# The norm behind a mixture of experts, run under its last expert

## The reference

```python
def layer_norm(x, g, b):
    mu = jnp.mean(x, -1, keepdims=True)
    var = jnp.mean(jnp.square(x - mu), -1, keepdims=True)
    return (x - mu) * lax.rsqrt(var + LN_EPS) * g + b

def expert_choice_moe(x, w_router, w_gate_up, w_down):        # 16 experts, 128 tokens each
    aff = jax.nn.softmax(x @ w_router, axis=-1)
    gates, idx = lax.top_k(jnp.swapaxes(aff, 1, 2), cap)
    xs = x[bi, idx]
    g, u = jnp.split(jnp.einsum('becd,edf->becf', xs, w_gate_up), 2, axis=-1)
    out = jnp.einsum('becf,efd->becd', jax.nn.silu(g) * u, w_down) * gates[..., None]
    return jnp.zeros_like(x).at[bi, idx].add(out)

for layer in range(2):
    mix = windowed_gqa_sink(x, ...) if layer == 0 else bidir_rglru_block(x, ...)
    x = layer_norm(ALPHA * x + mix, ln_mix_g[layer], ln_mix_b[layer])
    ffn = expert_choice_moe(x, ...)
    x = layer_norm(ALPHA * x + ffn, ln_ffn_g[layer], ln_ffn_b[layer])
```

## Time and profile before

| | |
|---|---|
| median of 3 runs | 4395.35 us (4392.49 to 4397.17) |
| the profiled execution's own time | 4396.59 us |
| its span | 4394.9 us |
| PE busy | 4060.1 us (92%) |
| DVE, ACT, POOL busy | 35%, 24%, 7% |
| granted clock of PE, mean | 0.961 |
| DVE's copy of a hidden half (L3369), mean | 0.42 us |
| PE's transposes of X in the recurrent stage (L2325), eight tiles | 8.64 us |
| first weight load for the last turn of a hidden half, second MoE (L3157) | 4345.92 us |

### The profile page before, as it was taken

One profiled execution on the slowest core, in us unless ns is written; L12 is line 12 of the kernel. 1 busy time (PEld: TensorE's weight loads), 2 busy tenths in 40 slices (PEclk: granted clock), 3 DMA queues, 4 the chain that ended last, 5 costly groups with the idle time before them and its releaser, 6 DMA issues. The chain is left out here.

```text
span 4394.9 us, 65767 instructions
## 1 busy us (share of the span) xinstructions
PE 4060.1 (92%) x28648; PEld 2291.3 (52%) x28648; DVE 1535.3 (35%) x3424; ACT 1043.9 (24%) x2054; POOL 288.3 (7%) x348
## 2 busy tenths in 40 slices
PE   7999898999999979998987999998799878999996
PEld 4555575586868754544544444443344344444442
DVE  2345233445454531125647311111445538111112
ACT  2233121333333310104541000001244421000002
POOL 0000000101011100000110000000000110000000
PEclk9999899999999989999997999999899998999998
DMA  3000101100000031112017899995211137899995
GB/s 95 25 25 6 50 13 43 30 4 26 8 21 8 7 108 58 49 19 49 1 74 264 295 315 323 307 328 189 66 34 34 48 144 270 286 324 306 326 313 182
DMA packets 316878, 557.26 MB, mean 127 GB/s; under 512 B 47488, under 2 KB 127520, under 8 KB 316592
## 3 DMA queue, kind: packets, MB, share of 16 engines
q1 hardware_dynamic: 302992, 502.73, 33.8%
q0 software_dynamic: 9216, 33.56, 3.3%
q10 hardware_dynamic: 4384, 16.78, 1.0%
HBM read 508.95 MB, written 44.04 MB: 126 GB/s over the span
## 5 line engine op out<-in xcount | busy, mean ns | idle before, releaser
L3164 PE MATMUL bank<-ring,m_picked_T 128*128 128x512 f32 x2048 | 900.0, 598 | 4.1 <-ACT m_picked_T L3240 4.1
L3164 PEld LDWEIGHTS bank<-ring,m_picked_T 128*128 128x128 f32 x2048 | 389.8, 192 | 483.3 <-issue 477.7
L3164 PE MATMUL bank<-ring,m_hidden_T 128*128 128x512 f32 x1024 | 454.6, 592 | 0.0
L3164 PEld LDWEIGHTS bank<-ring,m_hidden_T 128*128 128x128 f32 x1024 | 189.9, 190 | 216.2 <-issue 216.2
L1401 PE MATMUL bank<-hnT,w_block 128*128 128x336 f32 (+3 forms) x800 | 272.9, 491 | 18.3 <-DMA w_block<-in_w_in 18.3
L375 PE MATMUL bank<-hnT,w_block 128*128 128x512 f32 (+3 forms) x640 | 247.6, 522 | 5.1 <-DMA w_block<-in_w_in 5.1
L3363 DVE TENSOR_TENSOR m_hidden<-m_hidden,bank 128x512 f32<-128x512 f32 x64 | 44.0, 688 | 560.4 <-ACT m_hidden L3249 560.4
L231 PE MATMUL bank<-xT,w_block 128*128 128x512 f32 x512 | 220.5, 592 | 0.8 <-ACT xT L2334 0.8
L1401 PEld LDWEIGHTS bank<-hnT,w_block 128*128 128x128 f32 x800 | 149.8, 193 | 107.3 <-issue 23.7
L2240 PE MATMUL bank<-out_w,out_in 128*128 128x512 f32 x384 | 166.7, 597 | 18.6 <-DMA out_w<-in_w_out 18.6
L3249 ACT ACTIVATE m_hidden<-bank 128x512 f32<-128x512 f32 x64 | 38.2, 597 | 550.0 <-PE bank L3164 550.0
(11 more groups left out here) (466 smaller groups left out, 5669.1 us busy)
## 6 DMA issues: line engine op xcount, KB each, us to landing
ring<-in_moe_w_gate_up SPq DMA_DIRECT2D x512, 512.0 KB, 7.7
ring<-in_moe_w_down SPq DMA_DIRECT2D x256, 512.0 KB, 4.6
w_block<-in_w_in SPq DMA_DIRECT2D x42, 512.0 KB, 3.9
x_rows<-X ACTq DMA_DIRECT2D x2, 4096.0 KB, 16.5
ring<-y_rows SPq DMA_DIRECT2D x16, 512.0 KB, 6.9
w_block<-in_lru_w_in SPq DMA_DIRECT2D x16, 512.0 KB, 4.0
out_in<-mix SPq DMA_DIRECT2D x8, 768.0 KB, 6.1
out_w<-in_w_out SPq DMA_DIRECT2D x6, 1024.0 KB, 13.9
```

Source lines behind the costliest of these rows:

```text
L3164: m = pe.matmul(banks[j][:, :], lhsT[:, (i % 8) * P:(i % 8 + 1) * P], ring[:, i, j, :], start=i % 8 == 0, stop=i % 8 == KD - 1)
```

## The change

In both layers, SP loads the eight row tiles of y_rows when the scatter of expert 14 (the 15th of 16) has landed and the slot's slab of the last expert is used. The norm of the eight tiles is written into the last expert's instruction streams of ACT and DVE, in an order fixed by hand; it works in place in X. Each finished tile is stored, to out in layer 1 and to x_rows in layer 0. The last expert's rows get a path of their own: POOL gathers its 128 rows of y_rows (the sum of 15 experts) into xg, DVE adds the gated result from PSUM to them (which takes the place of the scaling), the 128 rows are normed as one tile, and POOL scatters them over the stored tiles, now without an addition, when all eight stores have landed. In layer 0, SP then loads X back from x_rows in eight DMAs, and the transposes of the recurrent stage wait for each tile. A helper row_sum(t) is ACT's row sum, row_root(t) the three instructions for the inverse root, centre(t) DVE's mean and centred row (with the row sum for tiles 3 and 7), and settle(t) the last product. The removed norm_vector and norm_scalar are those of the kernel before.

```diff
@@ -66,6 +66,7 @@
         self.nc, self.phases = nc, 0
         self.constants_done = Tally(ctx.enter_context(nc.semaphore("constants_done")))
         self.router_in = Tally(ctx.enter_context(nc.semaphore("router_in")))
+        self.x_in = [Tally(ctx.enter_context(nc.semaphore(f"x_in_again{t}"))) for t in range(NT)]
         self.swaps = [[Tally(ctx.enter_context(nc.semaphore(f"{name}{layer}"))) for name in ("gathered", "scattered")]
                       for layer in range(2)]
...
@@ -2319,6 +2323,8 @@
     def tensor(pe):
         for i in range(2 * NT):
             t, h = i // 2, i % 2
+            if x_in and h == 0:
+                pe.wait_ge(*x_in[t].now())
             if i >= 8:
                 pe.wait_ge((odd if h else even).sem, i // 2 - 3)
             for b in range(4):
@@ -3018,7 +3024,7 @@
         setup_sync(nc.sync)
         setup_gpsimd(nc.gpsimd)
-        transpose_x(nc, c, ps, X, xT, st)
+        transpose_x(nc, c, ps, X, xT, st, k.x_in)
         setup_scalar(nc.scalar)
         setup_vector(nc.vector)
         sync(nc.sync)
...
@@ -3068,6 +3075,9 @@
         ln_in, y_in, total = st.sem("ln_in"), [st.sem(f"y_in{t}") for t in range(NT)], [st.sem(f"total{i}") for i in range(2)]
         mean, squared, varied, rooted, scaled, stored, out_done = (st.sem(n) for n in (
             "mean", "squared", "varied", "rooted", "scaled", "stored", "out_done"))
+        last_added, last_chain, last_squared, last_rooted, last_done = (st.sem(n) for n in (
+            "last_added", "last_chain", "last_squared", "last_rooted", "last_done"))
+        dst, lst = x_rows if out is None else out[0], st.sb("m_last_stats", [P, 6])
         grown, y_out, eps = st.sem("grown"), [st.sem(f"y_rows_out{i}") for i in range(2)], st.sb("ln_eps", [P, 1])
         def slab(e, i):
@@ -3241,20 +3251,37 @@
                 if e == 0:
                     ac.activation(xs[:, 512:1024], ps[5][:, :], ACT.Copy).then_inc(*x_odd.up())
+            def sigmoid(e, h):
+                ac.wait_ge(used.sem, SLABS * e + 8 * (h + 1))
+                ac.activation(hid[:, HALF_FF * h:HALF_FF * h + HALF_FF], ps[2 * h][:, :], ACT.Sigmoid).then_inc(*sig.up())
+            def copy_hidden(e, h):
+                ac.wait_ge(h_turned.sem, 2 * e + h + 1)
+                ac.activation(hs[:, 512 * h:512 * h + 256], ps[4][:, 256 * h:256 * h + 256], ACT.Copy).then_inc(*h_even.up())
+            def row_sum(t):
+                if not DVE_SUM(t):
+                    ac.wait_ge(y_in[t].sem, 16)
+                    if total[0].n:
+                        ac.wait_ge(*total[0].now())
+                    ac.activation(junk_row[0], row(t), ACT.Copy, accum_out=stat[t][:, 3:4]).then_inc(*total[0].up())
+            def row_root(t):
+                s = stat[t]
+                ac.wait_ge(mean.sem, t + 1)
+                ac.activation(junk_row[1], row(t), ACT.Square, bias=s[:, 0:1], accum_out=s[:, 1:2]).then_inc(*squared.up())
+                ac.wait_ge(*squared.now())
+                ac.activation(s[:, 1:2], s[:, 1:2], ACT.Ln, bias=eps[:, :], scale=1.0 / D).then_inc(*varied.up())
+                ac.wait_ge(*varied.now())
+                ac.activation(s[:, 2:3], s[:, 1:2], ACT.Exp, scale=-0.5).then_inc(*rooted.up())
             copy_tokens(0)
             scaled_rows()
-            for e in range(NE):
+            for e in range(NE - 1):
                 for h in range(2):
-                    ac.wait_ge(used.sem, SLABS * e + 8 * (h + 1))
-                    ac.activation(hid[:, HALF_FF * h:HALF_FF * h + HALF_FF], ps[2 * h][:, :],
-                                  ACT.Sigmoid).then_inc(*sig.up())
-                    ac.wait_ge(h_turned.sem, 2 * e + h + 1)
-                    ac.activation(hs[:, 512 * h:512 * h + 256], ps[4][:, 256 * h:256 * h + 256],
-                                  ACT.Copy).then_inc(*h_even.up())
-                if e < NE - 1:
-                    copy_tokens(e + 1)
-                else:
-                    ac.preload_act_table_set("natural_log_exp_and_others")
+                    sigmoid(e, h)
+                    copy_hidden(e, h)
+                copy_tokens(e + 1)
                 ac.wait_ge(used.sem, SLABS * (e + 1))
                 if e:
                     ac.wait_ge(scattered.sem, 16 * e)
@@ -3262,6 +3289,32 @@
                     ac.wait_ge(y_out[1].sem, 16 * NT // 2)
                 ac.wait_ge(picked.sem, 2 * min(e + 1, FAST + 1))
                 ac.activation(ys[:, 0:512], ps[6][:, :], ACT.Copy, scale=gates[:, e:e + 1]).then_inc(*y_even.up())
+            e = NE - 1
+            sigmoid(e, 0)
+            ac.preload_act_table_set("natural_log_exp_and_others")
+            row_sum(0)
+            row_sum(1)
+            row_root(0)
+            row_sum(2)
+            row_root(1)
+            copy_hidden(e, 0)
+            row_root(2)
+            row_sum(4)
+            row_root(3)
+            sigmoid(e, 1)
+            ac.preload_act_table_set("natural_log_exp_and_others")
+            row_sum(5)
+            copy_hidden(e, 1)
+            row_root(4)
+            row_sum(6)
+            for t in range(5, NT):
+                row_root(t)
+            ac.wait_ge(last_chain.sem, 2)
+            ac.activation(junk_row[1], xg[:, :], ACT.Square, bias=lst[:, 3:4], accum_out=lst[:, 4:5]).then_inc(*last_squared.up())
+            ac.wait_ge(*last_squared.now())
+            ac.activation(lst[:, 4:5], lst[:, 4:5], ACT.Ln, bias=eps[:, :], scale=1.0 / D).then_inc(*last_rooted.up())
+            ac.wait_ge(*last_rooted.now())
+            ac.activation(lst[:, 5:6], lst[:, 4:5], ACT.Exp, scale=-0.5).then_inc(*last_rooted.up())
         def count_vector(ve, x, t, first, last, op, weight, slot):
@@ -3406,13 +3459,69 @@
             ve.tensor_copy(gates[:, FAST:], ps[2][:, NE + FAST:2 * NE]).then_inc(*picked.up())
             copy_tokens(2)
             scale_out(1)
-            for e in range(FAST, NE):
+            for e in range(FAST, NE - 1):
                 for h in range(2):
                     act(e, h)
                     copy_hidden(e, h)
-                if e < NE - 1:
-                    copy_tokens(e + 1)
+                copy_tokens(e + 1)
                 scale_out(e)
+            def centre(t):
+                s = stat[t]
+                if DVE_SUM(t):
+                    ve.wait_ge(y_in[t].sem, 16)
+                    ve.tensor_reduce(s[:, 3:4], row(t), AX.X, ALU.add).then_inc(*total[1].up())
+                    ve.wait_ge(*total[1].now())
+                else:
+                    ve.wait_ge(total[0].sem, t + 1 - (t + 1) // 4)
+                ve.tensor_scalar(s[:, 0:1], s[:, 3:4], -1.0 / D, None, ALU.mult).then_inc(*mean.up())
+                ve.wait_ge(*mean.now())
+                ve.scalar_tensor_tensor(X[:, t, :], row(t), s[:, 0:1], g, ALU.add, ALU.mult).then_inc(*scaled.up())
+            def settle(t):
+                ve.wait_ge(rooted.sem, t + 1)
+                ve.wait_ge(scaled.sem, t + 1)
+                ve.scalar_tensor_tensor(X[:, t, :], X[:, t, :], stat[t][:, 2:3], b, ALU.mult, ALU.add).then_inc(*stored.up())
+            e = NE - 1
+            ve.wait_ge(ln_in.sem, 32)
+            centre(0)
+            act(e, 0)
+            centre(1)
+            settle(0)
+            centre(2)
+            settle(1)
+            copy_hidden(e, 0)
+            centre(3)
+            settle(2)
+            centre(4)
+            settle(3)
+            act(e, 1)
+            centre(5)
+            copy_hidden(e, 1)
+            settle(4)
+            centre(6)
+            settle(5)
+            centre(7)
+            settle(6)
+            settle(7)
+            ve.wait_ge(used.sem, SLABS * NE)
+            ve.wait_ge(gathered.sem, 16 * (NE + 1))
+            for h in range(2):
+                s = slice(512 * h, 512 * h + 512)
+                ve.scalar_tensor_tensor(xg[:, s], ps[6 + h][:, :], gates[:, e:e + 1], xg[:, s], ALU.mult, ALU.add,
+                                        accum_out=lst[:, h:h + 1]).then_inc(*last_added.up())
+            ve.wait_ge(*last_added.now())
+            ve.tensor_tensor(lst[:, 2:3], lst[:, 0:1], lst[:, 1:2], ALU.add).then_inc(*last_chain.up())
+            ve.wait_ge(*last_chain.now())
+            ve.tensor_scalar(lst[:, 3:4], lst[:, 2:3], -1.0 / D, None, ALU.mult).then_inc(*last_chain.up())
+            ve.wait_ge(*last_chain.now())
+            ve.wait_ge(scattered.sem, 16 * (NE - 1))
+            ve.scalar_tensor_tensor(ys[:, :], xg[:, :], lst[:, 3:4], g, ALU.add, ALU.mult).then_inc(*last_chain.up())
+            ve.wait_ge(*last_chain.now())
+            ve.wait_ge(last_rooted.sem, 2)
+            ve.scalar_tensor_tensor(ys[:, :], ys[:, :], lst[:, 5:6], b, ALU.mult, ALU.add).then_inc(*last_done.up())
         def gpsimd(gp):
             def gather(e):
@@ -3424,11 +3533,10 @@
             gp.wait_ge(rows_out.sem, 16)
             gp.wait_ge(picked.sem, 2)
             gather(0)
-            for e in range(NE):
-                if e < NE - 1:
```

(76 more changed lines are left out.)

4 lines of the change are left out of this document (1 added, 3 removed).

## The result

The changed kernel takes 4352.33 us (median of 4 runs, 4351.53 to 4353.24), the kernel before 4396.14 beside it (4 runs). The ratio is 0.9902, with a 95% interval from 0.9885 to 0.9919: 43.8 us faster, where 42.5 was forecast, and inside the range. The profiled execution took 4353.24 with a span of 4351.5.

The account below looks back on a forecast made before the run. Serial tails without matmuls after both MoEs (46.7 and 39.3 us) were taken as the removable time, with PE 92% busy. Savings of 24.3 and 18.2 make 42.5, from 4395.35 to 4353; range 4347 to 4364.

Parts of the forecast that it names:

- The moved norm: Eight-tile norm inside the last expert: inputs arrive without a wait, last settle ends at 4358.9, 2.5 us after PE.
- PE's stall: Last expert, second hidden half: PE waits about 0.8 us in each MoE for the late second act.
- The last scatter: Plain scatter of the last expert's rows: 5.16 us, taken from the gather; bounds 2.6 and 6.17.
- POOL's pick-up: Between the last tile's final product and the start of POOL's last scatter: 0.76 us.
- The last tile's norm: Norm of the last expert's rows after the last settle: 3.52 us plus a last product of 1.28.
- The end of the span: Second MoE, after the last scatter lands at 4369.6: 1.0 us remains, ending at 4370.6.
- the second tail: End of the second MoE to the span's end: 4370.6 against 4394.9, 24.3 us saved.
- The first tail: First MoE's end to the recurrent stage's projection, with X reloaded: 3090.0 against 3108.21, 18.2 us saved.
- The half-speed start of PE: In the projection after the first MoE: may add some 1.5 us.
- The clock: Rival: PE's clock falls in the last expert's stall, its 8.8 us of matmuls take double: 4371; chance 0.04.
- The reload: Rival: X's reload after the first MoE is slow or blocks the weights; half rate adds 11.8 us: 4365; chance 0.06.
- Row tile 0: Rival: its late landing delays PE, each microsecond past 4331 costing one per MoE; chance 0.03, of which 0.02 slower.

Follow-up runs that it names:

- e5: Changed kernel without the eight loads of X from x_rows and the wait for them, so X lacks the last expert's part: 4355.28 us (single run).
- e3: Changed kernel with the eight row loads issued from tile 7 down to tile 0 in both MoEs: 4375.88 us (single run).
- e9: Changed kernel with ACT summing tile 7, no POOL wait for its last scatter, and work behind the second act reordered: 4350.07 us (median of 4).
- e10: The changed kernel, unaltered, run again beside the reordered version: 4356.77 us (median of 4), ratio to the kernel before 0.9904.

## Why the prediction was right

**The moved norm.** Measured from the scatter of expert 14, forecast and found: first row sum 14.1 and 14.1; end of the second act 31.6 and 31.4; last settle 43.9 and 43.3; last product done 48.6 and 48.26 (4343.04 + 1.29). The list of DVE's work, summed start to start, was good to 0.2 us up to the second act (it starts from 4330.35, where 4329.10 + 1.15 gives 4330.25), and from settle 4 to the last settle 8.9 were forecast and 9.0 found. The 0.6 by which the last settle came early is the next point.

**PE's stall** was forecast as 0.8 and was 0.13 at the turn (4327.53, which is 31.46 after the scatter, against 31.33 before). The step that failed is the one that counted the stall from the first weight load: before, the load began 0.42 ahead of the turn, and now the turn begins 0.06 behind the end of the act. This stall was in the sum. The prediction let ACT's copy wait for the turn and settle 4 for the root behind that copy; the copy came 32.15 after the scatter where 32.9 was forecast, and settle 4 at 34.3 where 35.0 was forecast. So the 0.7 too much for the stall is what made the last settle 0.6 early.

**The last scatter** is the term that was mis-sized most. I took 5.16 from the gather and kept 2.6 as the bound below; the scatter's traffic and landing in the second MoE are (40 slices of 4344 to 4351.5 us; issue to landing):

```profile
GB/s 0 0 0 0 0 0 0 0 0 0 0 284 371 371 502 371 393 437 66 0 0 0 0 0 0 0 0 0 0 0 0 0 0 0 0 0 0 0 0 0
...
out<-m_ys,m_tokens POOLq DMA_INDIRECT x1, 3.4
```

It is 3.4, nearer to the plain write than to the gather. The gather of the earlier trace rows was a poor neighbour: POOL was idle, but the DMA engines were not. The kernel before has gathers alone on the queues, the first of each MoE. The slices from 0.2 us ahead of the gather, first that of the earlier trace rows, then the first of the second MoE (3646.71), 7.2 us each:

```profile
GB/s 273 296 250 296 250 319 273 341 296 341 341 296 273 319 228 250 319 364 319 364 387 250 159 137 91 68 68 0 0 0 0 0 0 0 0 0 0 0 0 0
m_picked<-x_rows,m_tokens POOLq DMA_INDIRECT x1, 5.2
```

```profile
GB/s 0 0 0 0 0 0 0 0 0 0 159 159 23 91 46 273 364 341 387 501 387 182 46 0 0 0 0 0 0 0 0 0 0 0 0 0 0 0 0 0
m_picked<-x_rows,m_tokens POOLq DMA_INDIRECT x1, 4.3
```

By these rows, half of the 1.8 us too much came from a row taken under other traffic, and half from a gather lasting longer than a plain scatter. The estimate from the Trainium skill, "DMA: Bandwidth & Descriptors", section "Latency and other measured facts", was 4.3, and this too is above the measurement, by less. It had added the first byte's 1 us to the fixed 2 us, which the section does not say to do; without it the estimate is 3.3. POOL's pick-up was 0.27 (4344.33 to 4344.60) instead of 0.76. The last tile's norm took 5.0 from the last settle, where 4.8 was forecast.

**The end of the span** hid that error. I had 1.0 us from the last landing to the end, taken from a store by SP. The span ends 3.5 us after the scatter's landing (4348.0), with 2.9 of it SP's wait in the barrier. At the landing I was 2.7 too late (1.8 the flight, 0.5 the pick-up, 0.4 the norm), and here 2.5 too early; that the second tail was forecast at 24.3 and found at 24.5 is the luck of two errors of nearly the same size.

**The first tail.** The same 2.7 us came early at the landing, 51.9 after the scatter of expert 14 where 54.6 was forecast. From the landing to the projection I had 14.4 and it took 15.9, because I let X be complete when its traffic ends (11.8 after the issue) and the last tile's turn begins 13.8 after it. In the sum it was w_block that set the start, 2.6 behind X (the 14.4); it came 2.1 behind the last turn's start, which makes the 15.9. Forecast 18.2, found 19.4. Here too an error too late, of 2.7, and one too early, of 1.5, partly cancel. The barrier ended 4.7 after the landing, where 5.0 was forecast (3.69 of issues and 1.29); POOL's lateness, which the forecast did not know, hid behind SP's issues. The last turn and its copies were put at 1.6, where the terms named (8.64 / 8 and 0.69) give 1.8, and took 1.8 (3081.99 to 3083.81); the sum did not use it. The half-speed start of PE, for which the prediction allowed 1.5 in the projection, fell on the transposes instead: the granted clock is 0.50 until 3076 and 1.00 when the projection begins at 3084.09. That the reload costs 1.8 net was not in the forecast and is e5's.

**The rivals.** The clock did not fall in the last expert, and e3 shows that it does in a longer stall. The reload was not slow: the last three tiles' turns begin 1.3 us apart (3079.33, 3080.65, 3081.99), which is 0.5 MB at some 390 GB/s, as in the earlier trace rows. Row tile 0 was not late. ACT's first row sum began at the end of the table load without a wait, and e3 gives the price if it had been late: about 24 us for a tile that came 11.3 and 11.4 late in the two MoEs.

## What to carry to other kernels

When a serial tail is written into the streams of engines that wait, sum their work start to start up to each instruction that the busy engine needs, and then to the end. That one engine ends last (here DVE, 2.6 us behind PE) does not make stalls of the busy engine free: follow its path back, since it may, as here, wait on the way for work that the busy engine releases. Take the price of a transfer from a row under the same traffic. A tail that ends in a DMA issued by POOL should be given its own price at the following barrier. Check whether a removed transfer leaves two other waits of nearly the same length, as here the barrier and the transposes, before expecting its duration back.

## What the runs showed of the hardware

The routing stage ahead of the experts took 62.1 to 62.3 or 65.0 to 65.3 us in the first MoE, and 61.7 to 62.1, 64.7 to 65.2 or 67.9 to 68.0 in the second, in kernels in which its code is the same; either length of the first stood with each of the second's three but one (62 with 65). PE's granted clock differs with it. The kernel before, two routing stages (length, busy of PE, PEld, DVE, ACT, POOL, granted clock, DMA share, GB/s):

```profile
2285.50:2350.60 65.10, 42.68 (x242) 30.54 (x242) 27.82 (x172) 13.32 (x41) 0.30 (x3) 0.71 0.68 259
3584.80:3646.70 61.90, 39.56 (x242) 29.31 (x242) 27.74 (x172) 13.43 (x41) 0.28 (x3) 0.78 0.71 272
```

The changed kernel:

```profile
2285.50:2347.70 62.20, 39.80 (x242) 29.46 (x242) 27.82 (x172) 13.41 (x41) 0.33 (x3) 0.77 0.71 271
3559.80:3627.70 67.90, 45.56 (x242) 31.96 (x242) 27.63 (x172) 13.30 (x41) 0.33 (x3) 0.70 0.65 248
```

The same 242 PE records take 42.7 or 39.6 us before, 39.8 or 45.6 after, with the mean clock between 0.70 and 0.78. These 6 us lie in neither tail. The first 15 experts of the first MoE vary too, with the stage ahead of them: from the first gather to the scatter of expert 14 they took 668.2 to 668.6 us behind a routing stage of 62, and 669.9 to 670.4 behind one of 65, in the old form and in the new. The profiles of e9 and e10 differ by 16.0 us in span, of which 4.6 lie in the tails, 9.2 in the routing stages and 1.8 in these experts. Such differences are large enough for the spread of e10's runs, 4345.98 to 4359.31; since each kernel has one profile, it is not shown that they make it. What sets which length a stage gets was not settled.

With the DMA engines otherwise idle, a plain scatter of 128 rows of 4 KB landed in 3.3 to 3.4 us (the last of each MoE), a gather of the same size in 4.3 to 4.5 (the first of each MoE in the kernel before), and the accumulating scatter in 6.2 (4357.09 in the kernel before). Beside other traffic of 0.77 MB the gather took 5.2. An all-engine barrier behind the landing of POOL's scatter kept SP waiting 2.9 us, with POOL's own wait for the landing left out 1.5, and 0.2 behind a store by SP.
